# The 32 sampled tokens' products of the mixing and output stages, moved to four column groups of TensorE

## What is computed

```python
g_a, g_b = jnp.split(jax.nn.sigmoid(u_gate), 2, axis=-1)
mixed = (g_a * (o_a.reshape(B, T, W_A) @ p_a) + g_b * (o_b @ p_b)) @ w_o
x = x + mixed
x = x + hier_moe(rmsnorm(x, norm_ffn), w_grp, w_exp, we_gate, we_up, we_down)
```

## Time and profile before

| | us |
|---|---|
| median of 3 runs | 1974.67 (1972.24 to 1978.53) |
| span of the profiled execution | 1970.6 |
| mixing stage, from 1256.8 to 1414.5 | 157.7 |
| output and routing, from 1414.5 to 1597.5 | 183.0 |
| experts and final norm, from 1597.5 | 373.1 |

### The profile page before, as it was taken

How to read it: one execution, slowest core, us unless ns; L and a number is a source line. 1 busy time by engine, 2 the same in 40 slices (tenths; PEclk the granted TensorE clock), 3 DMA queues, 4 the chain that set the end, 5 groups by cost and what they waited for, 6 DMA issues and landing times. The chain is left out here.

```text
span 1970.6 us, 35644 instructions
## 1 busy us (share of the span) xinstructions
PE 1773.7 (90%) x15302; PEld 1058.4 (54%) x15302; DVE 694.5 (35%) x1541; ACT 396.1 (20%) x821; POOL 221.2 (11%) x218
## 2 busy tenths in 40 slices
PE   6999889879999699999999999799999839999980
PEld 4654455548788566666766666464555413333320
DVE  3212456532555723233333323224322421111116
ACT  3001344422232211111111111112010101111112
POOL 2000466520000000000000000000000131111100
PEclk9999999999999899999999999889899859999995
DMA  5601899871100011011111010442430049999946
GB/s 197 221 1 62 282 333 363 324 266 33 32 33 28 7 54 42 27 45 35 38 45 42 27 42 17 189 155 66 151 151 33 33 168 350 397 396 406 391 166 274
DMA packets 83902, 291.66 MB, mean 148 GB/s; under 512 B 16521, under 2 KB 25609, under 8 KB 73217
## 3 DMA queue, kind: packets, MB, share of 16 engines
q1 hardware_dynamic: 63312, 228.59, 30.9%
q0 software_dynamic: 19280, 56.53, 7.9%
q10 hardware_dynamic: 1152, 4.26, 0.6%
HBM read 253.69 MB, written 43.50 MB: 151 GB/s over the span
## 5 line engine op out<-in xcount | busy, mean ns | idle before, releaser
L1284 PE MATMUL gate_p<-rows,gate_w 128*128 128x352 f32 x768 | 280.7, 486 | 1.4 <-DMA gate_w<-in_w_in 1.4
L1047 PE MATMUL rw_pp<-rows,rw_w 128*128 128x264 f32 x896 | 204.3, 389 | 8.4 <-DMA rw_w<-in_w_in 8.4
L1047 PEld LDWEIGHTS rw_pp<-rows,rw_w 128*128 128x128 f32 x896 | 170.6, 191 | 40.4 <-DMA rw_w<-in_w_in 8.6
L1284 PEld LDWEIGHTS gate_p<-rows,gate_w 128*128 128x128 f32 x768 | 129.4, 189 | 55.4 <-issue 2.4
L1961 PE MATMUL x_p<-late 128*128 128x512 f32 (+1 forms) x288 | 128.7, 601 | 2.6 <-PEq L182 2.6
L2230 PE MATMUL moe_gu<-wgu,rows 128*32 128x512 f32 (+1 forms) x640 | 125.0, 617 | 2.8 <-DMA wgu<-in_we_gu 1.5
L2230 PE MATMUL moe_gu<-late,rows 128*32 128x512 f32 (+1 forms) x640 | 122.6, 599 | 0.0
L1506 DVE TENSOR_TENSOR tl<-tl,scan_zb 128x256 f32<-128x256 f32 x64 | 26.9, 421 | 192.9 <-PE scan_zb L1298 192.9
L1961 PEld LDWEIGHTS x_p<-late 128*128 128x128 f32 (+1 forms) x288 | 51.6, 184 | 67.4 <-issue 67.4
L1438 ACT COPY ys<-scan_yp 128x256 f32<-128x256 f32 x80 | 29.8, 372 | 222.9 <-PE scan_yp L1298 222.9
L2230 PEld LDWEIGHTS moe_gu<-wgu,rows 128*32 128x32 f32 (+1 forms) x640 | 30.2, 117 | 71.8 <-issue 60.6
(11 more groups left out here) (404 smaller groups left out, 2884.4 us busy)
## 6 DMA issues: line engine op xcount, KB each, us to landing
wgu<-in_we_gu SPq DMA_DIRECT2D x16, 2048.0 KB, 14.2
late<-in_we_gu SPq DMA_DIRECT2D x16, 2048.0 KB, 10.7
wd<-in_we_down SPq DMA_DIRECT2D x16, 1024.0 KB, 9.8
late<-in_we_down SPq DMA_DIRECT2D x16, 1024.0 KB, 12.5
rows<-in_cache_v SPq DMA_DIRECT2D x44, 256.0 KB
gate_rows<-u_rw SPq DMA_DIRECT2D x60, 176.0 KB, 1.9
rows<-in_cache_kT SPq DMA_DIRECT2D x34, 256.0 KB
mix_gate<-gate_rows SPq DMA_DIRECT2D x16, 528.0 KB, 4.1
```

The lines of the kernel that those rows point to most:

```text
L1047: mm = pe.matmul(pp[u % 2][:, c, 0:QN], w[:, n % 2, k, :], e.xnT[:, k, at:at + QN], start=(i == 0), stop=(i == KD - 1))
L1284: mm = pe.matmul(out[:, 0:GATE_N], gw[:, j % 2, k, :], e.xnT[:, k, at], start=(k == 0), stop=(k == KD - 1))
```

## The change

In the mixing stage the sampled tokens' products swap operands. The 32 tokens' 128 x 32 slice of k becomes the stationary operand, and the weights of four blocks stream, 512 columns. The four k-slices don't accumulate; each goes to column group k of PE, so to 32 PSUM partitions of its own in `parts_p` (`sample_parts`). ACT copies the four parts to SBUF (`keep_parts`), and `sum_parts` multiplies each block's 128 columns of them with `select`, a 128 x 32 matrix of four stacked identities, which sums over k and turns the result to features on partitions, as before, in `sp_bank`. There are four such sets: two in branch a, ahead of the products of blocks 3 and 7, and two in branch b, ahead of blocks 6 and 7; each is summed behind its block's products. The bank for the parts is taken from the products (NBK = 3), and `wa` has five slots, so that four blocks' weights are there at once. DVE makes `select` at the start of the stage.

In the output stage the last tile's part 0 now takes all eight k-slices, in four column groups (slices k and k+4 accumulate in one group), into the last tile's bank pair. DVE copies one column half of it to SBUF, ACT the other, and part 1 is two products with `select`, one for each half.

```diff
-    NBK, HN = 4, SEQ // 2
+    NBK, HN = 3, SEQ // 2
...
-        wa, wb = sb("mix_wa", [P, 2, HP, P]), sb("mix_wb", [P, KD, HP, P])
+        wa, wb = sb("mix_wa", [P, WA, HP, P]), sb("mix_wb", [P, KD, HP, P])
...
+        parts_p = ps("mix_sample_rows", [P, 512])
...
-            def sample_product(g, j, weights, src):
-                for k in range(HP):
-                    mm = pe.matmul(sp_bank[:, g, j], weights[:, k], src[:, k, SEQ:NT], start=(k == 0), stop=(k == HP - 1))
-                return mm
+            def sample_parts(v, blocks, src):
+
+                if v:
+                    pe.wait_ge(parts_kept, v)
+                at = 0
+                for weights in blocks:
+                    n = weights.shape[1]
+                    for k in range(HP):
+                        mm = pe.matmul(parts_p[NS * k:NS * (k + 1), at:at + n * P], src[:, k, SEQ:NT], weights[:, :, k],
+                                       start=True, stop=True)
+                    at += n * P
+                mm.then_inc(parts_made, 1)
+
+            def sum_parts(v):
+
+                pe.wait_ge(select_set, 1)
+                pe.wait_ge(parts_kept, v + 1)
+                for j in range(HP):
+                    mm = pe.matmul(sp_bank[:, v // 2, v % 2 * HP + j], parts[:, j * P:(j + 1) * P], e.select[:],
+                                   start=True, stop=True)
+                mm.then_inc(parts_summed, 1)
...
-                pe.wait_ge(wa_loaded[j % 2], 16 * (j // 2 + 1))
-                mm = sample_product(0, j, wa[:, j % 2], e.oaT)
+                pe.wait_ge(wa_loaded[j % WA], 16 * (j // WA + 1))
+                if j == 3:
+                    sample_parts(0, (wa[:, 0:4],), e.oaT)
+                if j == 7:
+                    sample_parts(1, (wa[:, 4:5], wa[:, 0:3]), e.oaT)
...
+                if j == 3:
+                    sum_parts(0)
+                if j == 7:
+                    sum_parts(1)
...
+                if j >= KD - 2:
+                    pe.wait_ge(obs_ready, 1)
+                    h = j - KD + 2
+                    sample_parts(2 + h, (wb[:, 4 * h:4 * h + 4],), e.obT)
...
-            pe.wait_ge(obs_ready, 1)
-            for j in range(KD):
-                mm = sample_product(1, j, wb[:, j], e.obT)
-            mm.then_inc(sample_made, 1)
+                if j >= KD - 2:
+                    sum_parts(j - KD + 4)
...
+            def keep_parts(v):
+                act.wait_ge(parts_made, v + 1)
+                if v:
+                    act.wait_ge(parts_summed, v)
+                act.copy(parts[:], parts_p[:]).then_inc(parts_kept, 1)
...
+                if r in (5, 9, KD + 7):
+                    keep_parts((5, 9, KD + 7).index(r))
...
+            keep_parts(3)
...
+            def out_last(part):
+
+                if part == 0:
+                    pe.wait_ge(added, LAST - 1)
+                    for c in range(2):
+                        for k in range(KD):
+                            at = slice(k % 4 * NS, k % 4 * NS + NS)
+                            mm = pe.matmul(xp[LAST % 2][at, c], e.mixedT[:, k, SEQ:NT], wo[:, k, c * 512:(c + 1) * 512],
+                                           start=(k < 4), stop=(k >= 4))
+                        mm.then_inc(last_made, 1)
+                else:
+                    pe.wait_ge(added, LAST)
+                    for c in range(2):
+                        pe.wait_ge(last_kept[c], 1)
+                        mm = pe.matmul(xp[1 - LAST % 2][0:NS, c], e.select[:], last[:, c], start=True, stop=True)
+                    mm.then_inc(made, 1)
...
+                    act.wait_ge(last_made, 2)
+                    act.copy(last[:, 1], xp[LAST % 2][:, 1]).then_inc(last_kept[1], 1)
                     exps(0)
...
+                if t == LAST - 1:
+                    dve.wait_ge(last_made, 1)
+                    dve.tensor_copy(last[:, 0], xp[LAST % 2][:, 0]).then_inc(last_kept[0], 1)
                 dve.wait_ge(h_turned, t + 1)
```

More of the change, by code:

```diff
@@ L1576, in stage_mix @@
     st = e.steps["dve"]
+    WA = 5
     e.rw_mem.close()
@@ L1583, in stage_mix @@
     e.wr = e.late[:, KD * (NT + D):].rearrange("p (k n) -> p k n", k=KD)
+    e.select = e.mix_mem.enter_context(nc.sbuf_tensor("select", [P, NS], F32))
     next_loaded, table_zero, gain_loaded, table_set = (sem("wo_loaded"), sem("table_zero"), sem("rs_gain_loaded"),
                                                        sem("table_set"))
-    wa_loaded, wb_loaded = [sem(f"mix_wa_loaded{b}") for b in range(2)], sem("mix_wb_loaded")
+    wa_loaded, wb_loaded = [sem(f"mix_wa_loaded{b}") for b in range(WA)], sem("mix_wb_loaded")
+    select_set, parts_made, parts_kept, parts_summed = (sem("mix_select_set"), sem("mix_parts_made"), sem("mix_parts_kept"),
+                                                        sem("mix_parts_summed"))
     g_loaded = [sem(f"mix_gate_loaded{b}") for b in range(2)]
     made, gated, summed, used = sem("mix_made"), sem("mix_gated"), sem("mix_summed"), sem("mix_used")
-    sample_made, ob_ready, prods = sem("mix_sample_made"), sem("mix_ob_ready"), sem("mix_prods")
+    ob_ready = sem("mix_ob_ready")
     state_loaded, state_done, stored = sem("rs_state_loaded"), sem("rs_state_done"), sem("rs_stored")
@@ L1604, in stage_mix @@
         part = sb("mix_part", [P, 2, HN])
+        parts = sb("mix_sample_parts", [P, 512])
         empty = sb("empty", [P, NE * e.CAP // P * 4], I32)
@@ L1734, in _ @@
             for j in range(KD):
-                pe.wait_ge(wa_loaded[j % 2], 16 * (j // 2 + 1))
-                mm = sample_product(0, j, wa[:, j % 2], e.oaT)
-                for h in range(2):
-                    product(2 * j + h, wa[:, j % 2], e.oaT)
+                pe.wait_ge(wa_loaded[j % WA], 16 * (j // WA + 1))
[3 more added lines that the diff above has]
+                    sample_parts(1, (wa[:, 4:5], wa[:, 0:3]), e.oaT)
+                for h in range(2):
+                    product(2 * j + h, wa[:, j % WA], e.oaT)
+                if j == 3:
+                    sum_parts(0)
+                if j == 7:
+                    sum_parts(1)
                 if j + 1 < KD:
@@ L1858, in branch_b @@
                 dve.tensor_tensor(mixed, mixed, part[:, m % 2], ALU.add).then_inc(summed, 1)
+            st.then(dve, dve.tensor_tensor(e.select[:], e.c("ident")[:, 0:NS], e.c("ident")[:, NS:2 * NS], ALU.add))
+            st.then(dve, dve.tensor_tensor(e.select[:], e.select[:], e.c("ident")[:, 2 * NS:3 * NS], ALU.add))
+            dve.tensor_tensor(e.select[:], e.select[:], e.c("ident")[:, 3 * NS:4 * NS], ALU.add).then_inc(select_set, 1)
             for n in range(2 * KD):
@@ L1883, in _ @@
             mixed_s = e.mixedT[:, :, SEQ:NT]
-            dve.wait_ge(sample_made, 1)
+            dve.wait_ge(parts_summed, 2)
             dve.wait_ge(gated, KD)
@@ L1894, in _ @@
                     finish()
-            dve.wait_ge(sample_made, 2)
+            dve.wait_ge(parts_summed, 4)
             dve.wait_ge(gated, 2 * KD)
@@ L1914, in stage_out_and_route @@
     ent_ready, scattered, w_early = sem("ent_ready"), sem("scattered"), sem("moe_w_early")
+    last_made, last_kept = sem("wo_last_made"), [sem(f"wo_last_kept{c}") for c in range(2)]
+    LAST = NTT - 1
     e.moe_w = e.ctx.enter_context(ExitStack())
@@ L1924, in stage_out_and_route @@
         junk = e.beside_x1[:, 0:D]
+        last = e.beside_x1[:, D:2 * D].rearrange("p (c n) -> p c n", c=2)
         stat = sb("h_stat", [P, 3, NTT])
@@ L1995, in _ @@
                 if t + 1 < NTT:
-                    out(t + 1, 0)
+                    out(t + 1, 0) if t + 1 < LAST else out_last(0)
                 turn(t)
                 if t + 1 < NTT:
-                    out(t + 1, 1)
+                    out(t + 1, 1) if t + 1 < LAST else out_last(1)
                 logits(t)
```

6 lines of the change are left out of this document (3 added, 3 removed).

## The result

The changed kernel takes 1957.26 us (median of 4 runs, 1955.99 to 1959.94), the kernel before 1973.45 (4 runs, 1971.71 to 1978.53): a ratio of 0.9923, 95% interval 0.9904 to 0.9942. The span of its profiled execution is 1955.1 us, 15.5 less than before. The medians differ by 16.2 us (by the interval, 11 to 19).

A forecast was written before the change was run, and what follows sets the result against it. PE's own order of work was taken to bound the mixing and output stages. The terms -5.3 - 4.5 + 0 - 2.4 = -12.2 us, with span 1970.6 and 4.1 around it, gave 1962.5 us, range 1956.5 to 1970.

The forecast's parts named there:

- A: Mixing stage, first half: eight sample sets removed, two part sets and two selection sets added; -5.3 us.
- B: Mixing stage, second half: shorter tail behind the last product, with DVE late next; -4.5 us.
- C: Start of the output stage: half-clock time might give -1.8 or +1 us; taken as 0.
- D: Last tile of the output stage: logits up to 5.2 us earlier, limited by the clock; middle taken, -2.4 us.
- term of 4.1 us: Added to the span for what lies around it: median run 1974.67 us against the profiled span of 1970.6.
- the prediction's alternative (A = -3.7): Mixing, first half: half-clock sets worth only 0.91 us each, because light work no longer draws the slow time; -3.7 us.
- covered add_state wait: Mixing, first half: the selection set covers PE's wait for DVE's add_state before a last small product; 0.3 us gained.
- cases of -0.9 and -3.5: Last tile: clock falls ahead of turn(7), -0.9 us; or falls during turn(7) and returns for the logits, -3.5.
- Groups one after the other: Rival: column groups run in turn, a set costing 3.43 in place of 0.86 us; sum +1.5, 1976.2 us; chance 0.05.
- Weight loads not overlapped: Rival: eight 32-column weight loads add 0.9 us a set; sum -10.9, 1963.8 us; chance 0.04.
- The late copy: Rival: in mixing PE stands 5.8 us for ACT's copy and loses 1.8 of clock; -4.6, 1970.1 us; chance 0.05.
- The first rival: Clock and cover give back more: D = -0.9, C = +1, A = -3.7; sum -8.1, 1966.6 us; chance 0.22.

The follow-up runs named there:

- first pair: The first two profiles, of the kernel before and the changed kernel; spans 1970.6 and 1955.1 us.
- e7_changed_again: The changed kernel, unedited, run again on another occasion; 1959.61 us, ratio 0.9935 to the kernel before.
- e5_three_banks: Kernel before with three banks for the prompt's products in place of four, nothing else; 1970.84 us, ratio 0.9993 to the kernel before.
- e1: Kernel before with only the output stage's part of the change, selection matrix made at the start of mixing; 2001.31 us, ratio 0.9989 to the kernel before.
- e2: Changed kernel with the output stage of before, so only the mixing stage's part; 1997.17 us, ratio 0.9957 to the kernel before.
- e4: Changed kernel with the last tile's 32 four-group passes made twice, filling PE's idle time before turn(7); 1991.49 us, ratio 0.9921 to the kernel before.
- e8: Changed kernel with DVE's norm of tile 7 ahead of the expert choice, which is cut into three pieces; 1953.76 us, ratio 0.9907 to the kernel before.
- e3: Changed kernel with mixing's four k-slices accumulating in one column group, operands still swapped; 2005.68 us, ratio 0.9996 to the kernel before.
- e6: Changed kernel with ACT's first copy of the parts behind gate row 5 in place of gate row 4; 1969.44 us, one run.

## Why the prediction was right

**The sum.** It forecast -12.2 us. The touched stretches of the first pair give -12.4, those of e7_changed_again against e5_three_banks -14.2, and the medians -16.2 at first and -12.3 with e7_changed_again. The mechanisms came as written: the groups at once, DVE late next at the end of mixing, turn(7) held by DVE, the clock at half behind it. That the sum fits so well is partly luck, since its terms missed both ways. The table has the stretches of all profiles that bear on each term ("without" and "with" that term's part of the change; the rows from the second to C have the profiles of row A, in its order). One pair of profiles alone misleads by about 1 us a term, because the clock rises and falls at other places each time.

| us | without this part | with it | forecast | difference of means |
|---|---|---|---|---|
| A | 88.2, 89.1, 89.0 (before, e1, e5) | 82.8, 82.6, 81.8, 81.6, 82.6 (changed, e2, e4, e7, e8) | -5.3 | -6.5 |
| block 0 to block 1 | 12.0, 12.8, 12.8 | 11.1, 10.9, 10.2, 10.1, 11.0 | -1.7 | -1.8 |
| state products | 9.2, 8.5, 8.6 | 7.8, 7.9, 8.5, 8.6, 7.9 | 0 | -0.6 |
| block 2 to block 3 | 11.4, 12.1, 12.1 | 10.4, 10.2, 9.6, 9.5, 10.3 | -1.7 | -1.9 |
| B | 65.2, 64.6, 64.6 | 61.1 or 61.2 in all | -4.5 | -3.6 |
| C | 132.1, 132.8, 132.8 | 131.8, 131.7, 133.0, 133.0, 131.7 | 0 | -0.3 |
| D | 17.4 in all (before, e5, e2) | 14.9, 13.7, 13.8, 13.8, 13.7 (changed, e1, e3, e7, e6) | -2.4 | -3.4 |

**The time.** 1962.5 was 5.2 us too high. 3.3 of that is the span, 15.5 us shorter in place of 12.2, of which 3.1 lie in stages that the change leaves alone (e2_mix_only, e5 to e8 show their start of mixing to vary by 2 us and more without it). Another 2.5 is the term of 4.1 us for what lies around the span. It compared one run's span with the median of three runs: the changed kernel's profiled run took 1956.72 us for its span of 1955.1, which is 1.6, and every run whose span is on record has 1.6 to 1.8. The remaining 0.5 goes the other way, the median of the changed kernel's runs against its profiled one.

**Term A, -5.3, measured -5.4 in the first pair and -6.5 over all profiles.** The part sets cost 1.00 us each, the second no more than the first (forecast 1.0 and 1.1), the selection sets 0.90 and 0.81 (0.91). In the first pair the two sets at half clock seem not to be worth 1.72 us, as in the prediction's alternative (A = -3.7): the clock returned 5.2 us after PE's start with the set or without it (1264.7 before, 1262.7 after), and blocks 0 and 2 became shorter by 0.8 and 1.0 us only. What makes up for it there is the state products, 1.4 us shorter, because the clock fell 4.1 us into them and not 2.3. The other profiles don't bear this out. Here is the same part of e5_three_banks, with the old form:

```profile
1258.95 1.92 PE L1668 MATMUL mix_sample<-rows,mix_wa 128*128 128x32 f32 x8 [3.97 <-DMA mix_wa<-in_p_ab]
...
1279.66 8.55 PE L1690 MATMUL rs_xo<-sample_cols,rows 64*64 64x8 f32 x128
...
1301.23 1.08 PE L1668 MATMUL mix_sample<-rows,mix_wa 128*128 128x32 f32 x8
```

and of e7_changed_again:

```profile
1259.89 8.68 PE L1669 MATMUL mix_b<-rows,mix_wa 128*128 128x512 f32 x16 [4.22 <-DMA mix_wa<-in_p_ab]
...
1277.06 8.61 PE L1713 MATMUL rs_xo<-sample_cols,rows 64*64 64x8 f32 x128
...
1296.07 1.06 PE L1680 MATMUL mix_sample_rows<-mix_wa,rows 128*32 128x512 f32 x8
```

From the start to block 3 it is 42.3 against 36.2 us, 6.1 less, with equal state products; the three sets that are gone there were priced at 4.35. In e1 and e5 the clock returned 6.8 us after PE's start, in the seven profiles with part sets 3.2 to 5.2. So the price of 1.72 us a set isn't refuted; in the mean blocks 0 and 2 gave 1.8 and 1.9. Of the 1.2 us by which the term was under, half is what the sum put at nothing, the state products; the rest is 0.3 for those two blocks and 0.3 for the cheaper selection sets and the end of branch a. With three profiles of the old form that split is rough. The 0.3 us of covered add_state wait came true: PE's wait of 0.31 us there is no longer in the list of waits.

**Term B, -4.5, measured -4.1 in the first pair and -3.6 over all.** The end comes at +2.68 us behind the last product (forecast 2.6) in the changed kernel, and within 0.01 of it in e2, e4, e7 and e8, set by DVE as forecast. Two sizes were off. The removed tail was taken from a profile in which the clock fell 5.1 us into the sample set, 9.98 us; in e1 and e5 it fell at 5.9 and 5.8 and the tail was 9.3. And the three sets between the products hold PE for 2.9 us as forecast, but the products beside them take 0.3 more: 6.97 us for each of blocks 6 and 7 and 27.56 for the four ahead of them, 41.50 in place of 41.20. That is about 0.1 us at each change of form, which the prediction didn't count on the products' side. The missing bank is excluded by e5_three_banks.

**Terms A and B together.** Mixing as a whole was 144.5 to 145.6 us in the five profiles with its change (changed, e2, e4, e7, e8) and 155.0 to 155.3 in the three without, 10.1 us apart in the mean, where A and B promise 9.8: the two misses cancel.

**Term C, 0, measured -0.3.** The clock did fall between the stages, and PE had 3.0 us of half clock in place of 3.7; in the other profiles it had 2.8 to 5.5 us with the change and 5.1 and 5.2 without.

**Term D, -2.4, measured -2.5 in the first pair, but -3.6 or -3.7 in e1, e3, e6 and e7.** PE gained nothing ahead of turn(7), which waited 3.8 us for DVE in all five, as forecast. In the first pair turn and selection ran at half clock and the logits didn't, between the prediction's cases of -0.9 and -3.5; in the other four the clock fell just ahead of turn(7) and came back inside the selection products. So the close hit is luck: the usual value is that of the case put at -3.5. e4_twice gives the upper bound that the prediction worked out, 5.2 us, and shows that the clock is what the rest of the term hangs on.

**The rivals.** Groups one after the other: excluded by the 1.00 us and, as a counter-trial, its price confirmed by e3_one_group, 3.55 us a set (forecast 3.43 and 0.15 for the form). Weight loads not overlapped: a set would take 1.9 us. The line of the Trainium skill (TensorE: Matmul & The Clock Gate, "Part 3: Packing small matmuls — row/col tiling") that loads overlap only across row groups doesn't describe this kernel: loads into other column groups were hidden in all four sets. The same section also lets a load into the background weight buffer go ahead of running products; that would fit, but no run here shows which it was. The late copy: didn't happen; made to happen by e6_late_copy, it cost 9.7 us, where the rival had 5.8 us of standing and 1.8 of clock. The first rival's low bounds: none came true. A gained more than its forecast and wasn't at -3.7, C not at +1, and D never at -0.9.

## What to carry to other kernels

In this kernel, swapping small products that stream few columns paid only because the column groups then ran at once: one group gave nothing and four gave 10 us. Before moving work off the busiest engine, look for what it waits for next; in the last tile more than half of the 8.8 us freed (14.0 less 3.4 and 1.8) were first given to a wait for DVE and a slow clock, and putting DVE's urgent instruction ahead of its long chain won 2.6 to 3.6 us more. Compare untouched stretches of two profiles before crediting a change with their difference, and take a stretch that the clock passes through from several profiles: here one pair gave -5.4 and -2.5 us for two terms whose means were -6.5 and -3.4. And take what lies around the span from a run whose own time and span are both known.

## What was not expected

Adding 3.4 us of superfluous products in front of a waiting instruction made the last tile's stretch 1.4 to 2.6 us shorter (e4_twice), as the clock stayed at its upper level (2.4 GHz). The kernel before took 2004.84 us in the median on one chip and 1971.93 on another; the profiles of its variants on the first reach PE's first product of the mixing stage after 1292 to 1298 us, on the second after 1257 to 1261, so the difference of 33 us lies in the stages ahead of it. Why isn't known.
